# A two-layer sequence block and a mixture of experts on one core: six of eight xbc blocks in three passes, first taps on ScalarE, other work moved around them

## The chip, the cores and the metric

The kernel runs on one core of a Trainium2 chip. The metric is the device time of one execution in microseconds; the time before is the median of 3 runs. The engines are TensorE (matmul, here PE), VectorE (DVE), ScalarE (ACT), GpSimd (POOL) and SyncE (SP), which issues the weight loads.

## The reference

```python
for i in range(DEPTH):                                   # DEPTH = 2, SEQ = 256, D_MODEL = 1024
    x = x + 0.5 * swiglu(rms_norm(x, ffn1_norm[i]), ...)
    h = rms_norm(x, mix_norm[i])
    proj = h @ w_in[i]
    z, xbc, dt_raw, q, k, v = jnp.split(proj, splits, axis=-1)
    xbc = jax.nn.silu(causal_depthwise_conv(xbc, conv_w[i], conv_b[i]))   # 4 taps, 2048 channels
    y_ssd = ssd_mixer(xbc, dt_raw, z, dt_bias[i], a_log[i], d_skip[i], ssd_norm[i])
    ...
    y_att = dilated_attention(q, k, v).reshape(b, s, ATT_WIDTH)
    x = x + jnp.concatenate([y_ssd, y_att], axis=-1) @ w_out[i]
    x = x + 0.5 * swiglu(rms_norm(x, ffn2_norm[i]), ...)
# then a second block: mod = silu(c) @ w_ada (8 pieces of 1024), a gated linear attention with a
# convolution branch, and 32 experts of width 512 of which each token takes two
```

All values are float32. `ssd_mixer` takes step sizes `dt = softplus(dt_raw + dt_bias)`, turns them into decays and scans two chunks of 128 tokens.

## The kernel before

Activations lie transposed in SBUF: 128 channels on the partitions, 256 tokens along the row. A weight block is 1024 x 256, 1 MB, in one of four ring slots (`ring`). SyncE loads the block four places on as soon as TensorE has counted `freed` for the slot. The four PSUM banks of `misc` are taken in turn by every "fill"; `claim_bank` waits until the bank's last content is `drained`. Each engine works its own list of instructions in order, and the lists are written out by hand in one function for each engine.

**Two ways to multiply.** `cols_out` (line 930) multiplies a float32 block by `xnT` in one product; the trace shows it as two records for each 128 x 128 weight tile. The other way, in `three` (lines 779 to 781), splits both sides into a high part in fp32r and the rest: high by low, low by high, high by high. For that ScalarE copies the block into a high part (`high_w_block`, line 1810; three homes in turn, so a copy waits until the block three before has been read) and VectorE subtracts it from the block into `ring_low` (`low_w_block`, line 2390). The activations need `xh` (line 1802) and `xl` (line 2410).

**The xbc stage.** Behind the norm TensorE computes eight blocks of xbc (16 chunks of 128 channels). With `X_SPLIT = 4` blocks 0 to 3 go by `cols_out`, 4 to 7 by three passes; block 7 carries the step sizes dt beside it (line 993). Then come z's first block, the turns of x to tokens (line 1003, 16 transposes in four banks), the turns of B (line 1008), two more blocks of z, the cumulative decays (lines 1015, 1016, they wait for `adt_ready`), z's last block and the q, k and v blocks.

VectorE scales each evacuated xbc block by `row_rstd` (line 2416) and convolves four chunks at a time (a quartet, q = 0 to 3): the first tap with the bias (line 2426), then three taps of four instructions (line 2432). ScalarE takes the SiLU of a finished quartet (`conv_silu`, line 1814). Behind the last quartet VectorE reads dt (line 2445), which drains its bank, and ScalarE evacuates z's first block (line 1819), copies the token turns (line 1841), and takes Exp and Ln of the step sizes (lines 1849, 1852).

**Modulation pieces.** GpSimd sums eight pieces of `mod` over the stretch of the feed-forward blocks; `modulation(p)` on TensorE is 16 records with one column each (line 1164), and VectorE adds the bias (line 2642). In layer 0's second feed-forward block pieces 2 and 3 stand ahead of the last `down`, in layer 1's two blocks one piece each. The last `down` sums its two column halves one after the other and tells VectorE of the first (`acc_half`), which adds both to x (`add_x`, line 2374). Behind it TensorE turns x for the next norm (line 801).

## Time and profile before

| | |
|---|---|
| median of 3 runs | 2113.42 us (2113.1 to 2113.86) |
| the profiled execution | 2112.5 us, its span 2110.7 us |
| TensorE busy | 2069.4 us, 98% |
| VectorE busy | 1642.4 us, 78% |
| ScalarE busy | 1179.5 us, 56% |
| GpSimd busy | 454.9 us, 22% |

Times in the rows are microseconds from the start of the span. The xbc stage runs from 201.7 to 266.8 in layer 0 and from 834.9 to 898.2 in layer 1. Matmuls overlap, so their pace is read from start to start and not from their durations.

### The profile page before, as it was taken

The numbers are of one execution on the slowest core, as the hardware profiler recorded it, in microseconds if no ns is written. First come the engines' busy times: TensorE is split into PE (matmuls) and PEld (weight loads), VectorE is DVE, ScalarE is ACT, GpSimd is POOL, SyncE is SP. The second block draws the span as 40 slices with busy tenths as digits, with TensorE's granted clock in tenths as the row PEclk, the third lists the DMA queues.
The fourth block names the chain that finished last, engine by engine and source line by source line (L and its number), as shares of the span: only waits on it lengthen the run. The fifth ranks groups of instructions, "written<-read, shape, count | busy, mean of one in ns | idle before, by whom it ended". The sixth has DMA issues, their size and how long they took to land. (4 is left out here: it accounts for less than half of the span.)

```text
span 2110.7 us, 35271 instructions
## 1 busy us (share of the span) xinstructions
PE 2069.4 (98%) x13609; PEld 1845.2 (87%) x13609; DVE 1642.4 (78%) x2095; ACT 1179.5 (56%) x1483; POOL 454.9 (22%) x237
## 2 busy tenths in 40 slices
PE   9999999999999999999999999999999999999997
PEld 8998999789999998999789998999877878777775
DVE  5775867567766875867567766888699999999998
ACT  5433365653435433365653435344378888888886
POOL 4991000007931990000007930000000000000000
PEclk9999999999999999999999999999999999999999
DMA  8874554247765774554347753445669999999994
GB/s 261 282 253 159 160 160 141 100 142 243 265 226 164 266 257 152 163 154 140 101 143 244 265 184 120 132 125 174 243 231 369 366 372 368 375 370 372 374 369 180
DMA packets 238936, 483.66 MB, mean 229 GB/s; under 512 B 10612, under 2 KB 178976, under 8 KB 222464
## 3 DMA queue, kind: packets, MB, share of 16 engines
q1 hardware_dynamic: 226880, 443.58, 60.0%
q0 software_dynamic: 11360, 37.21, 5.3%
q10 hardware_dynamic: 608, 1.65, 0.2%
q8 instruction: 60, 0.98, 0.2%
q14 instruction: 28, 0.23, 0.0%
HBM read 481.31 MB, written 1.09 MB: 229 GB/s over the span
## 5 line engine op out<-in xcount | busy, mean ns | idle before, releaser
L780 PE MATMUL misc<-xh,ring_low 128*128 128x256 f32 x1472 | 407.4, 277 | 0.0
L779 PE MATMUL misc<-xl,high_b 128*128 128x256 f32 x1344 | 372.7, 277 | 0.0
L781 PE MATMUL misc<-xh,high_b 128*128 128x256 f32 x1344 | 371.8, 277 | 0.0
L2998 DVE TENSOR_TENSOR ring_low<-ring,high_b 128x2048 fp32r<-128x2048 f32 x128 | 287.1, 2284 | 0.6 <-issue 0.6
L780 PEld LDWEIGHTS misc<-xh,ring_low 128*128 128x128 f32 x1472 | 277.0, 188 | 3.5
L1766 ACT ACTIVATE arena<-arena 128x256 f32<-128x256 f32 x88 | 36.8, 419 | 416.9 <-DVE arena L2343 416.9
L2306 DVE TENSOR_TENSOR ring_low<-ring,high_b 128x2048 fp32r<-128x2048 f32 x88 | 255.6, 2940 | 9.3 <-ACT high_b L1735 8.7
L779 PEld LDWEIGHTS misc<-xl,high_b 128*128 128x128 f32 x1344 | 252.3, 188 | 3.4
L781 PEld LDWEIGHTS misc<-xh,high_b 128*128 128x128 f32 x1344 | 252.4, 188 | 0.0
L2056 ACT ACTIVATE high_b<-ring 128x2048 fp32r<-128x2048 f32 x124 | 235.7, 1914 | 27.8 <-DMA ring<-in_w_dram 26.9
L1648 POOL TENSOR_SCALAR arena<-arena,cact 128x1024 f32<-128x1024 f32 x56 | 213.0, 3804 | 3.9 <-DMA arena<-in_w_ada_dram 0.9
L1412 PE MATMUL misc<-high_b,ue 128*128 128x512 f32 x512 | 204.2, 399 | 1.9 <-DVE ue L3041 1.2
L1414 PE MATMUL misc<-ring_low,ue 128*128 128x512 f32 x512 | 199.9, 390 | 0.0
L1645 POOL TENSOR_SCALAR arena<-arena,cact 128x1024 f32<-128x1024 f32 x4 | 14.9, 3719 | 731.4 <-DVE hidl L2328 724.3
L1735 ACT ACTIVATE high_b<-ring 128x2048 fp32r<-128x2048 f32 x88 | 163.5, 1904 | 6.3 <-DMA ring<-in_ffn_w_up_dram 4.5
L779 PE MATMUL misc<-ring_low,xh 128*128 128x256 f32 x512 | 146.0, 285 | 2.4 <-DVE arena L2486 2.4
L3004 DVE TENSOR_TENSOR ring_d_low<-ring_d,high_r 128x1024 fp32r<-128x1024 f32 x128 | 147.9, 1215 | 0.5
L2343 DVE TENSOR_TENSOR arena<-misc,row_rstd 128x256 f32<-128x256 f32 x88 | 37.0, 421 | 136.1 <-PE misc L781 125.5
L781 PE MATMUL acc<-high_r,hidh 128*128 128x512 f32 x352 | 139.6, 397 | 0.0
L2061 ACT ACTIVATE high_r<-ring_d 128x1024 fp32r<-128x1024 f32 x128 | 131.6, 1055 | 14.0 <-DMA ring_d<-in_w_dram 13.3
L780 PE MATMUL acc<-high_r,hidl 128*128 128x512 f32 x352 | 139.0, 395 | 0.0
L779 PE MATMUL acc<-ring_d_low,hidh 128*128 128x512 f32 x352 | 138.3, 393 | 0.0
(474 smaller groups left out, 5092.7 us busy)
## 6 DMA issues: line engine op xcount, KB each, us to landing
ring<-in_w_dram SPq DMA_DIRECT2D x128, 1024.0 KB, 7.7
ring<-in_w_in_dram SPq DMA_DIRECT2D x72, 1024.0 KB, 5.5
ring_d<-in_w_dram SPq DMA_DIRECT2D x128, 512.0 KB, 5.2
ring<-in_ffn_w_gate_dram SPq DMA_DIRECT2D x44, 1024.0 KB, 5.5
ring<-in_ffn_w_up_dram SPq DMA_DIRECT2D x44, 1024.0 KB, 8.9
ring_d<-in_ffn_w_down_dram SPq DMA_DIRECT2D x88, 512.0 KB, 7.5
arena<-in_w_ada_dram POOLq DMA_DIRECT2D x48, 512.0 KB, 5.1
ring<-in_w_out_dram SPq DMA_DIRECT2D x20, 1024.0 KB, 4.8
```

Source lines behind the costliest of these rows:

```text
L779: pe.matmul(dst, wh, ml, start=start, stop=False, **kw)
L780: pe.matmul(dst, wl, mh, start=False, stop=False, **kw)
L781: return pe.matmul(dst, wh, mh, start=False, stop=stop, **kw)
L1412: pe.matmul(b, ue[:, k, half, :], expert_part(high_b, x)[:, kk, :], start=(k == 0), stop=False)
L1414: mm = pe.matmul(b, ue[:, k, half, :], expert_part(ring_low, x)[:, kk, :], start=False, stop=(k == KD - 1))
L1648: pool.tensor_scalar(row, row, cact[:, k:k + 1], None, ALU.mult).then_inc(pool_step, 1)
L1735: act.activation(high_b[:, s, :], ring[:, s, :], ACT.Copy).then_inc(high_in[s], 1)
L2056: act.activation(high_b[:, s, :], ring[:, s, :], ACT.Copy).then_inc(high_in[s], 1)
L2061: act.activation(high_r[:, s, :], ring_d[:, s, :], ACT.Copy).then_inc(high_in_d[s], 1)
L2306: dve.tensor_tensor(ring_low[:, s, :], ring[:, s, :], high_b[:, s, :].bitcast(F32), ALU.subtract)\
L2998: dve.tensor_tensor(ring_low[:, s, :], ring[:, s, :], high_b[:, s, :].bitcast(F32), ALU.subtract)\
L3004: dve.tensor_tensor(ring_d_low[:, s, :], ring_d[:, s, :], high_r[:, s, :].bitcast(F32), ALU.subtract).then_inc(low_in_d[s], 1)
```

## The change

`X_SPLIT` becomes 6: xbc blocks 2 to 7 go in three passes. ScalarE makes `xh` and the high parts of blocks 2 and 3 (b = -6 and -5) before it loads the table for SiLU and copies `row_rstd`, and it takes the first tap with the bias of each quartet (`first_taps`), counted in a new semaphore `tap_in`, for which VectorE's other three taps wait. The order of VectorE's list is written anew: `xl` first, a low part behind each evacuation, the taps behind each second one; the reading of dt and `dn` stand ahead of the last quartet. ScalarE's last `conv_silu` moves behind z's first block and the token copies. Of two modulation pieces the second moves between the halves of the last `down`, on TensorE and on VectorE.

```diff
-        X_SPLIT = 4
+        X_SPLIT = 6
         SPLIT = [(RING[k], uses) for k, uses in slots if k[0] == "ffn" or k == "moe"]
         SPLIT += [(RING["win", l] + 8 - X_SPLIT, 16 + X_SPLIT) for l in range(DEPTH)]
...
-            def down(m0, n0, d0, g0, i, c, start, stop):
+            def down(m0, n0, d0, g0, i, c, start, stop, between=()):
...
                     if stop and (t, cc) == (1, 0):
                         mm.then_inc(acc_half, 1)
+                        for p in between:
+                            modulation(p)
                 mm.then_inc(freed_d[dn % SLOTS], 1)
...
-                for p in pieces:
+                for p in pieces[:1]:
                     modulation(p)
-                down(m0, n0, d0, NF * f, 0, NF - 1, False, True)
+                down(m0, n0, d0, NF * f, 0, NF - 1, False, True, pieces[1:])
...
                 n0 = RING["win", l]
                 root_of_squares(3 * l + 1)
-                rms(3 * l + 1, ACT.Silu)
-                act.wait_ge(rstd_ready, 3 * l + 2)
                 for q in range(4):
                     wait_drained(act, FILL["norm", 3 * l + 1] + q)
                 act.activation(xh[:, :, :], xnT[:, :, :], ACT.Copy).then_inc(xs_high, 1)
+                wait_summed(act, ROWD["ffn", 2 * l], 0, NF - 2)
+                wait_summed(act, ROWD["ffn", 2 * l], 0, NF - 1)
+                for b in (-6, -5):
+                    n = n0 + 8 + b
+                    act.wait_ge(loaded[n % SLOTS], LOAD * (n // SLOTS + 1))
+                    act.activation(high_w(b), ring[:, n % SLOTS, :], ACT.Copy).then_inc(high_in[n % SLOTS], 1)
+                rms(3 * l + 1, ACT.Silu)
+                act.wait_ge(rstd_ready, 3 * l + 2)
 
...
-                for j in range(8):
-                    wait_slot_read(act, n0 + j)
-                    if j < 3:
-                        high_w_block(j - 4)
-                    if j >= 4:
-                        high_w_block(j - 5)
-                    if j in (3, 5, 7):
-                        conv_silu(j // 2 - 1)
-                conv_silu(3)
+                def first_taps(q):
+                    for j in range(2 * q, 2 * q + 2):
+                        wait_drained(act, FILL["xbc", l] + j)
+                    for ch in range(4 * q, 4 * q + 4):
+                        at_ = C_CW + (CONV_K - 1) * NX + ch
+                        ins = act.activation(xc[:, ch, :], xraw[:, ch, CONV_K - 1:], ACT.Identity,
+                                             scale=cola[:, l, at_:at_ + 1], bias=cola[:, l, C_CB + ch:C_CB + ch + 1])
+                    ins.then_inc(tap_in, 1)
+
+                wait_slot_read(act, n0)
+                high_w_block(-4)
+                first_taps(0)
+                wait_slot_read(act, n0 + 1)
+                high_w_block(-3)
+                conv_silu(0)
+                wait_slot_read(act, n0 + 2)
+                high_w_block(-2)
+                first_taps(1)
+                wait_slot_read(act, n0 + 3)
+                high_w_block(-1)
+                conv_silu(1)
+                wait_slot_read(act, n0 + 4)
+                high_w_block(0)
+                first_taps(2)
+                wait_slot_read(act, n0 + 5)
+                high_w_block(1)
+                conv_silu(2)
+                wait_slot_read(act, n0 + 6)
+                first_taps(3)
+                high_w_block(2)
 
                 def z_out_of(j):
                     block_out(FILL["z", l, j], j, z[:, :, j * BLK:(j + 1) * BLK], ACT.Silu)
@@ -1840,6 +1870,7 @@
                     wait_filled(act, m)
                     act.activation(xtok[:, t, half * 512:(half + 1) * 512], bank_of(m), ACT.Copy)\
                         .then_inc(drained[m % 4], 1)
+                conv_silu(3)
                 m = FILL["bt", l]
                 wait_filled(act, m)
                 act.activation(btok.rearrange("p a b -> p (a b)"), bank_of(m), ACT.Copy)\
@@ -2358,14 +2389,16 @@
...
-                for p in pieces:
+                for p in pieces[:1]:
                     modulation(p)
-                add_x(u + 1, lambda t: half_rstd[:, t:t + 1], lambda: wait_summed(dve, d0, 0, NF - 1))
-
-            def add_x(u, factor, wait_last):
+                add_x(u + 1, lambda t: half_rstd[:, t:t + 1], lambda: wait_summed(dve, d0, 0, NF - 1), pieces[1:])
+
+            def add_x(u, factor, wait_last, between=()):
 
                 for c in range(2):
                     if c:
+                        for p in between:
+                            modulation(p)
                         wait_last()
                     else:
                         dve.wait_ge(acc_half, u)
...
-                for q in range(NX // 4):
-                    if q == 3:
-                        low_w_block(0)
-                    chunks = range(4 * q, 4 * q + 4)
-                    if q == 0:
-                        dve.wait_ge(row_ready, 3 * l + 2)
-                    if q == 2:
-                        low_w_block(-2)
-                    for j in range(2 * q, 2 * q + 2):
-                        if j == 1:
-                            dve.wait_ge(xs_high, l + 1)
-                            dve.tensor_tensor(xl[:, :, :], xnT[:, :, :], xh[:, :, :].bitcast(F32), ALU.subtract)\
-                                .then_inc(xs_low, 1)
-                        if j == 3:
-                            low_w_block(-3)
-                        m = FILL["xbc", l] + j
-                        wait_slot_read(dve, n0 + j)
-                        dve.tensor_tensor(xraw[:, 2 * j:2 * j + 2, CONV_K - 1:],
-                                          bank_of(m).rearrange("p (a b) -> p a b", a=2),
-                                          row_rstd[:, :].unsqueeze(1).to_broadcast([P, 2, SEQ]), ALU.mult)\
-                            .then_inc(drained[m % 4], 1)
+                dve.wait_ge(xs_high, l + 1)
+                dve.tensor_tensor(xl[:, :, :], xnT[:, :, :], xh[:, :, :].bitcast(F32), ALU.subtract)\
+                    .then_inc(xs_low, 1)
+                low_w_block(-6)
+
+                def raw(j):
+                    m = FILL["xbc", l] + j
+                    wait_slot_read(dve, n0 + j)
+                    dve.tensor_tensor(xraw[:, 2 * j:2 * j + 2, CONV_K - 1:],
+                                      bank_of(m).rearrange("p (a b) -> p a b", a=2),
+                                      row_rstd[:, :].unsqueeze(1).to_broadcast([P, 2, SEQ]), ALU.mult)\
+                        .then_inc(drained[m % 4], 1)
+
+                def convolve(q):
                     for j in range(2):
                         wait_drained(dve, FILL["xbc", l] + 2 * q + j)
-                    if q == 2:
-                        low_w_block(-1)
+                    dve.wait_ge(tap_in, 4 * l + q + 1)
                     last = {}
-                    for ch in chunks:
-                        last[ch] = step(dve.tensor_scalar(
-                            xc[:, ch, :], xraw[:, ch, CONV_K - 1:], taps(ch)(CONV_K - 1),
-                            cola[:, l, C_CB + ch:C_CB + ch + 1], ALU.mult, ALU.add))
                     for k in range(CONV_K - 1):
-                        for ch in chunks:
-                            after_step(last[ch])
+                        for ch in range(4 * q, 4 * q + 4):
+                            if k:
+                                after_step(last[ch])
                             ins = dve.scalar_tensor_tensor(out=xc[:, ch, :], in0=xraw[:, ch, k:k + SEQ],
                                                            scalar=taps(ch)(k), in1=xc[:, ch, :],
                                                            op0=ALU.mult, op1=ALU.add)
@@ -2436,9 +2458,26 @@
                                 last[ch] = step(ins)
                             else:
                                 ins.then_inc(conv_done, 1)
-                    if q == 0:
...
+
+                dve.wait_ge(row_ready, 3 * l + 2)
+                raw(0)
+                low_w_block(-5)
+                raw(1)
+                low_w_block(-4)
+                convolve(0)
+                raw(2)
+                low_w_block(-3)
+                raw(3)
+                low_w_block(-2)
+                convolve(1)
+                raw(4)
+                low_w_block(-1)
+                raw(5)
+                low_w_block(0)
+                convolve(2)
+                raw(6)
+                low_w_block(1)
+                raw(7)
                 m = FILL["dt", l]
                 wait_filled(dve, m)
...
                 wait_drained(dve, m)
                 dve.scalar_tensor_tensor(out=dn, in0=dr, scalar=-1.0, in1=dr, op0=ALU.mult, op1=ALU.min)\
                     .then_inc(dn_ready, 1)
-                for j in range(1, 4):
+                convolve(3)
+                for j in range(2, 4):
                     low_w_block(j)
                 dve.wait_ge(dl_ready, l + 1)
                 link(dve.scalar_tensor_tensor(out=dtv, in0=dr, scalar=0.0, in1=dl, op0=ALU.max, op1=ALU.add))
```

## Rows read from the trace of the kernel before

**Rows 1.** The page, section 1: busy time of each engine.
```profile
PE 2069.4 (98%) x13609; PEld 1845.2 (87%) x13609; DVE 1642.4 (78%) x2095; ACT 1179.5 (56%) x1483; POOL 454.9 (22%) x237
```
**Rows 2.** Windows: us; PE, PEld, DVE, ACT, POOL busy; granted clock; DMA share; GB/s.
```profile
202.00:205.50 3.50, 3.50 (x10) 2.77 (x9) 0.32 (x3) 2.38 (x5) 0.00 (x0) 0.52 0.00 0
636.10:639.00 2.90, 2.90 (x28) 2.89 (x26) 2.49 (x2) 2.88 (x3) 0.00 (x0) 1.00 0.98 336
639.10:645.80 6.70, 6.70 (x21) 5.43 (x21) 2.27 (x6) 1.38 (x2) 0.00 (x0) 0.50 0.68 236
827.00:836.00 9.00, 8.29 (x53) 6.97 (x52) 5.92 (x11) 3.41 (x7) 0.00 (x0) 1.00 0.74 231
```
**Rows 3.** Timeline of PE (start, us, what), pieces 2 and 3, layer 0.
```profile
635.87 0.39 PE L781 MATMUL acc<-high_r,hidh 128*128 128x512 f32 x1
636.10 1.84 PE L1164 MATMUL misc<-ones,arena 128*128 128x1 f32 x16
637.80 2.42 PE L1164 MATMUL misc<-ones,ada 128*128 128x1 f32 x16
...
641.51 0.63 PE L779 MATMUL acc<-ring_d_low,hidh 128*128 128x512 f32 x1
...
645.35 1.30 PE L801 MATMUL misc<-konst,x 128*128 128x128 f32 x8
```
**Rows 4.** Timeline of PE, the single piece of layer 1.
```profile
827.47 1.84 PE L1164 MATMUL misc<-ones,arena 128*128 128x1 f32 x16
```
**Rows 5.** Timeline of DVE, layer 0: the second half added to x.
```profile
645.59 1.41 DVE L2374 SCALAR_TENSOR_TENSOR x<-acc,stat,x 128x512 f32<-128x512 f32 x2 [1.08 <-PE acc L781]
```
**Rows 6.** Timeline of PE in the xbc stage of layer 1.
```profile
842.27 20.89 PE L930 MATMUL misc<-xnT,ring 128*128 128x256 f32 x96
862.80 0.47 PE L779 MATMUL misc<-xl,ue 128*128 128x256 f32 x1
...
879.67 0.29 PE L993 MATMUL misc<-wdt,xnT 128*128 128x16 f32 x2
...
894.05 1.03 PE L1003 MATMUL misc<-konst,arena 128*128 128x128 f32 x8
895.64 0.66 PE L1003 MATMUL misc<-konst,arena 128*128 128x128 f32 x4 [0.56 <-DVE arena L2445]
897.17 0.66 PE L1003 MATMUL misc<-konst,arena 128*128 128x128 f32 x4 [0.87 <-ACT arena L1819]
...
909.62 0.30 PE L1015 MATMUL misc<-arena,konst 128*128 128x32 f32 x2
```
**Rows 7.** Timeline of DVE in the same stage: evacuation, first tap, taps, low part.
```profile
872.24 0.68 DVE L2416 TENSOR_TENSOR arena<-misc,row_rstd 128x512 f32<-128x512 f32 x1
...
877.08 1.38 DVE L2426 TENSOR_SCALAR arena<-arena,cola 128x256 f32<-128x256 f32 x4
878.37 4.84 DVE L2432 SCALAR_TENSOR_TENSOR arena<-arena,cola 128x256 f32<-128x256 f32 x12
883.13 2.28 DVE L2390 TENSOR_TENSOR ring_low<-ring,ring_d_low 128x2048 fp32r<-128x2048 f32 x1
```
**Rows 8.** Timeline of ACT in the same stage.
```profile
837.94 1.28 ACT L1725 ACT_TABLE_LOAD   x1
...
879.58 1.92 ACT L1810 ACTIVATE ring_d_low<-ring 128x2048 fp32r<-128x2048 f32 x1 [2.54 <-PE misc L781]
...
904.30 0.23 ACT L1852 ACTIVATE arena<-arena 128x32 f32<-128x32 f32 x1
```
**Rows 9.** Line 1751, Identity on ScalarE: ns min/median/max, starts, form.
```profile
L1751 ACT ACTIVATE xnT<-misc,mod,gains x4: 557/566/570, 1279.7 to 1281.0; 128x256 f32<-128x256 f32 x4
```
**Rows 10.** The page, section 6: loads of w_in, KB each, median us to landing.
```profile
ring<-in_w_in_dram SPq DMA_DIRECT2D x72, 1024.0 KB, 5.5
```
**Rows 11.** GpSimd in layer 1's stage (windows), two low parts beside GpSimd (timeline).
```profile
834.00:930.00 96.00, 92.86 (x686) 88.67 (x687) 68.03 (x105) 47.06 (x55) 0.00 (x0) 1.00 0.47 143
...
596.34 6.68 DVE L2306 TENSOR_TENSOR ring_low<-ring,high_b 128x2048 fp32r<-128x2048 f32 x2
```

More of the change, by code:

```diff
@@ L425, in two_blocks @@
         xc_ready = sem("xc_ready")
+        tap_in = sem("tap_in")
         z_ready = sem("z_ready")
@@ L2438, in ssd_and_projections @@
                                 ins.then_inc(conv_done, 1)
-                    if q == 0:
-                        low_w_block(-4)
+                dve.wait_ge(row_ready, 3 * l + 2)
[17 more added lines that the diff above has]
+                raw(7)
                 m = FILL["dt", l]
```

## The prediction

> **What bounds the kernel now.** I read the page first: TensorE is busy for 98% of the span [rows 1]. Next I asked for the granted clock of single stretches, because a busy TensorE at half clock does half the work. Then came TensorE in order of time around the two places that the change touches, and last VectorE, ScalarE, the loads and GpSimd there, to see how far ahead of TensorE they run. Two things stand out.
>
> First, in the feed-forward block before layer 1, TensorE runs modulation(2) and modulation(3) back to back, 32 products of one column each. Behind them the clock is at half: 1.00 granted from 636.1 to 639.0, 0.50 from 639.1 to 645.8, that is 1.2 instead of 2.4 GHz [rows 2]. TensorE counts as busy all through this, so the waits don't show it. The spacing of matmuls does: the last nine of the down product take from 641.51 to 645.35, 0.43 us each, against 0.23 us ahead of the pieces [rows 3].
>
> Second, the xbc stage (the same in both layers; I use layer 1). Three blocks in one product take from 842.27 to 862.80, 6.84 us each. Then 147 matmuls of three-pass blocks take from 862.80 to 879.67, less 0.2 us before the second of them: 0.1135 us each, 5.45 us for a block's 48 [rows 6]. A three-pass block is the cheaper one, if its parts are ready. Behind z's first block come the turns to tokens, and two of them stand: the third four start 1.59 us after the first eight, which need 8 x 0.109 = 0.87, and the fourth four 1.53 us after the third, which need some 0.48. That is 0.7 and 1.05 us, 1.75 together. The rows name VectorE's step sizes (L2445) and ScalarE's z (L1819) as releasers [rows 6]: both stand in their queues behind the last taps.
>
> **The change, part by part.**
>
> *Piece 3 between the halves.* TensorE's instructions stay as they are; the order becomes piece 2, half, piece 3, half. At full clock a piece takes 1.70 us, from 636.10 to 637.80 [rows 3], and the twelve down matmuls 12 x 0.23 = 2.75 us plus about 0.1 us after each piece: 1.70 + 1.70 + 2.95 = 6.35 us, against the 9.25 us from 636.10 to 645.35 [rows 3]. Gain 2.9 us, if the clock stays up. The nearest row with a piece ahead of a down product and the turns after it is in layer 1, one piece from 827.47 on, down halves and turns behind it: 1.00 granted from 827 to 836 [rows 2, 4]. Two pieces with half a down product between them lie between that and the pair that fell, and nearer to the single piece, since dense work stands on each side of each piece. What is late next is x's second half: VectorE adds it at 645.59, 0.24 us behind 645.35, where the last product gives way to the turns [rows 3, 5]. It moves with that product, so the gain passes on whole. VectorE's own modulation(3) stands in front of that add, but piece 3 ends 1.4 us before it. In the other three feed-forward blocks nothing moves.
>
> *Blocks 2 and 3 in three passes.* Each saves 6.84 - 5.45 = 1.39 us of TensorE, 2.8 us for a layer [rows 6]. What must hide: ScalarE copies two more blocks (1.92 us each) and VectorE subtracts two more (2.28 us each) [rows 7, 8]. ScalarE makes its two ahead of row_rstd, right behind xh: three copies of about 1.85 us from 837.9 on, then the table load that stands at 837.94 before [rows 8], so row_rstd comes near 845.3 instead of 842.9. VectorE's first evacuation waits for it, and frees a bank that TensorE wants at about 860: nothing. VectorE has the first low part at 844.5 and the second at 848.4; TensorE wants them at 849.2 and 854.6.
>
> *First taps to ScalarE.* VectorE is relieved of 1.3 us for four chunks, from 877.08 to 878.37 [rows 7]. For two blocks it then has two evacuations of 0.6, two low parts of 2.2 and twelve taps in 4.75 us (starts to starts [rows 7]), 10.35 us, and TensorE takes 2 x 5.45 = 10.9. With the first taps kept it would be 11.65, and VectorE would be the bound. ScalarE's new instruction, Identity with a scale and a bias from memory, has its form in the second block's norm: 566 ns from PSUM [rows 9], 2.3 us for four and the upper bound; the lower is Ln's 0.23 us on a tile of 32 columns [rows 8], 0.9 us. I take 1.9, near the upper, whose row has the same shape and kinds of operands; either end changes only how long VectorE waits for tap_in. For two blocks ScalarE has 3.7 + 1.9 + 1.0 = 6.6 us of 10.9: free. A new wait arises: VectorE's taps wait for tap_in, and behind them stand the next evacuations and low parts.
>
> I followed the three queues through layer 1 by these durations, a load landing 5.5 us after its slot is free [rows 10]. Low parts are ready, against TensorE's want: block 4 at 852.3 for 860.1, block 5 at 859.9 for 865.6, block 6 at 864.6 for 871, block 7 at 872.2 for 876.5, z0 at 875.6 for 885.4, z1 at 883.2 for 893.5, z2 at 895.3 for 899.2. VectorE waits a few tenths for tap_in, 1.5 us in the last quartet. The smallest slack is some 4 us, at block 7 and z2. No new stall.
>
> *Step sizes and turns ahead of the last taps.* VectorE reads dt right after its last evacuation, near 886.6; ScalarE evacuates z's first block as soon as it ends (891.1 to 892.1), the last SiLU comes after the token copies. The third four turns (from 892.0) find their bank free, the fourth (from 892.4) too: the 1.75 us go. What is late next: ScalarE's Exp and Ln stand behind the copy of block 11. In the kernel before, Ln ends at 904.53 [rows 8], now near 900.8. adt is ready 0.5 us later; TensorE wanted it at 909.62 [rows 6] and now at 905.0: 3.6 us are left. The last chunks' SiLU at 895.1 is wanted behind z3, at 911. Nothing new.
>
> Sum for a layer: 2.8 + 1.75 = 4.5 us, twice 9.1; with 2.9 for the pieces 12.0 us. Later stages load and copy when TensorE frees a slot, so they move with it and should keep their time. The profiled execution took 2112.5 us (span 2110.7): 2100.5. The median of the runs is 0.9 us above it: **2101.4 us**.
>
> **Rivals.**
>
> *The clock falls all the same.* Behind the second half come sixteen transposes with a wait for x, as in layer 1 (832.4 to 835). For: in layer 0 one piece between transposes and a plain block went with 0.52 granted from 202.0 to 205.5 [rows 2]. Against: layer 1's single piece. A fall costs half of 3.5 to 6.7 us, 1.7 to 3.3: 2103 to 2105. The Trainium skill ("TensorE: Matmul & The Clock Gate", Part 4: PE-mode transpose) says that transposes don't count as busy work for the clock in the way that products do. By that rule the stretch behind piece 3 is thin, and this rival is what happens; layer 1's stretch with the same transposes, at 1.00, speaks against it. The same page (HAM oscillation) ties a fall to gaps in which TensorE is idle; the fall at 639 came with no gap at all, so here the trace decides.
>
> *The queues bite.* VectorE has only 10.9 - 10.35 = 0.55 us to spare for two blocks, and each wait for tap_in or for a copy (which waits for TensorE to read the block three before) eats of it. If waits of 2.5 us came in every quartet, VectorE would fall back by 1.95 us for each two blocks, 6.8 us from block 2 to z's first, 2.8 more than the slack of 4, and what the three passes save in a layer would go: 2101.4 + 5.6 = 2107.
>
> *Slower.* One mechanism: GpSimd working beside VectorE in the xbc stage. Two low parts that overlap GpSimd take 6.68 us from 596.34 [rows 11] instead of 4.5, so up to 4.4 for one against 2.2. At that pace two blocks cost VectorE 14.8 us against TensorE's 10.9, 3.9 behind for each pair, 13.6 over the 3.5 pairs to z's first block, 9.1 after a slack of 4.5, and 18 for both layers: 2119. It turns the sign at 6 us for a layer, that is where a low part takes more than some 4.0 us. Against: GpSimd has 0.00 us in the whole stretch [rows 11], and its next pieces are gated by feed-forward chunks.
>
> *Nothing in the end.* The stretch after the stage is set by VectorE or ScalarE and takes back what TensorE gained in the xbc stage: then the pieces alone remain, 2110.5, within 0.2%. For: adt's slack is only 3.6 us. Against: a copy there starts when TensorE has read a slot, so a TensorE that comes earlier is followed earlier; the only fixed chain is Exp and Ln, and it keeps its slack.
>
> **How the numbers follow.** Forecast 2101.4, 0.70, with 2099 to 2103.5 as its own range: a fall of the clock at the start of layer 0 can last 3.5 us or none, and a new wait of some tenths may stand at each of a dozen places. Clock falls 0.10, queues 0.12, nothing 0.05, slower 0.03. From 2098.5 to 2106 the forecast, the clock's case and part of the queues' are held. 0.2% is 4.2 us, about what a measurement of this kernel can tell from no change: faster than 2109.2 are the first three, 0.92; same 0.05; slower 0.03.
>
> **What would show it.** In the profile after: granted clock 1.00 from the first of the two pieces to the next gate product, and twelve down matmuls 0.23 us apart; plain blocks only two, from the third on 48 matmuls with 0.1135 us, no idle time before the first of block 2 to 7; no wait of the turns for L2445's or L1819's successors; z1 beginning 4.5 us earlier against block 0; VectorE with short waits for the new taps; Identity at 0.4 to 0.6 us without a table load. It would be wrong if TensorE waits for low parts, if adt comes after z2, or if 0.50 stands behind the pieces.

## The result and the profile after

The changed kernel takes 2101.41 us (median of four executions, 2098.96 to 2106.97) beside 2113.57 us for the kernel before (2113.10 to 2113.86): 0.9949 of it, 95% interval 0.9934 to 0.9964. The forecast was 2101.4 us, with 2099 to 2103.5 as its own range and 2098.5 to 2106 as the range held in all. The profiled execution of the changed kernel is its longest, 2106.97 us with a span of 2105.2.

The first line is the page's busy time (as [rows 1]), under it stretches from the windows view: us, busy time of PE, PEld, DVE, ACT and POOL, granted clock, DMA share, GB/s.

```profile
PE 2065.6 (98%) x13673; PEld 1847.7 (88%) x13673; DVE 1641.5 (78%) x2067; ACT 1203.2 (57%) x1519; POOL 455.8 (22%) x237
...
202.00:205.50 3.50, 3.50 (x19) 3.14 (x20) 0.53 (x4) 3.47 (x7) 0.00 (x0) 1.00 0.00 0
631.45:637.80 6.35, 6.35 (x46) 5.78 (x44) 4.65 (x6) 4.37 (x4) 0.00 (x0) 1.00 1.07 355
637.80:644.00 6.20, 5.21 (x40) 4.56 (x39) 5.68 (x11) 5.25 (x13) 0.00 (x0) 1.00 0.39 139
1269.80:1276.60 6.80, 6.80 (x22) 3.44 (x22) 1.43 (x4) 0.00 (x0) 1.16 (x2) 0.50 0.04 9
1515.60:1525.80 10.20, 10.20 (x50) 10.20 (x50) 5.44 (x20) 6.85 (x9) 0.92 (x2) 0.50 0.60 243
```

The clock stays at 1.00 through both pieces and behind them, where it fell before [rows 2]. It is also at 1.00 at 202, where the kernel before fell and where the change moves nothing on TensorE. And it falls, to 1.2 GHz, at 1269.8 and 1515.6, in parts of the program that the change doesn't touch. Such falls are one part of the scatter between executions and not all of it: the mean granted clock of seven executions of the kernel before, among thirty on one chip, was 0.994, and they took from 2112.1 to 2128.3 us.

The pieces in order of time (TensorE; answers [rows 3]):

```profile
631.45 1.84 PE L1167 MATMUL misc<-ones,arena 128*128 128x1 f32 x16
633.15 0.48 PE L780 MATMUL acc<-ring_d_low,hidh 128*128 128x512 f32 x1
...
634.62 1.84 PE L1167 MATMUL misc<-ones,ada 128*128 128x1 f32 x16
636.32 0.48 PE L780 MATMUL acc<-ring_d_low,hidh 128*128 128x512 f32 x1
...
637.80 1.03 PE L802 MATMUL misc<-konst,x 128*128 128x128 f32 x8
```

From 631.45 to 637.80 are 6.35 us, where [rows 3] have 9.25. The xbc stage of layer 1 on TensorE (answers [rows 6]):

```profile
834.23 0.61 PE L825 MATMUL acc<-konst,stat 128*128 128x128 f32 x4
834.67 7.07 PE L933 MATMUL misc<-xnT,ring 128*128 128x256 f32 x32
...
841.39 0.47 PE L780 MATMUL misc<-xl,ring_d_low 128*128 128x256 f32 x1
...
883.52 1.91 PE L1006 MATMUL misc<-konst,arena 128*128 128x128 f32 x16
885.26 0.60 PE L1011 MATMUL misc<-konst,arena 128*128 128x128 f32 x4
885.67 0.36 PE L780 MATMUL misc<-ring_low,xh 128*128 128x256 f32 x1
...
897.06 0.30 PE L1018 MATMUL misc<-arena,konst 128*128 128x32 f32 x2
```

One plain block is left behind the row of 1/rms (L825), and the sixteen turns (L1006) run in one group without a wait: 2.15 us from the first of them to z's next block, 4.19 before. VectorE and then ScalarE in the same stage (timelines; answer [rows 7, 8]):

```profile
863.27 2.28 DVE L2423 TENSOR_TENSOR ring_low<-ring,ue 128x2048 fp32r<-128x2048 f32 x1
...
873.22 0.69 DVE L2440 TENSOR_TENSOR arena<-misc,row_rstd 128x512 f32<-128x512 f32 x1
...
880.86 4.85 DVE L2454 SCALAR_TENSOR_TENSOR arena<-arena,cola 128x256 f32<-128x256 f32 x12 [1.82 <-ACT arena L1837]
...
893.17 0.26 DVE L2499 SCALAR_TENSOR_TENSOR arena<-arena 128x16 f32<-128x16 f32 x2
```

```profile
835.74 1.28 ACT L1728 ACT_TABLE_LOAD   x1
...
866.25 2.08 ACT L1837 ACTIVATE arena<-arena,cola 128x256 f32<-128x256 f32 x4 [0.59 <-DVE arena L2440]
...
878.64 2.08 ACT L1837 ACTIVATE arena<-arena,cola 128x256 f32<-128x256 f32 x4 [4.24 <-DVE arena L2440]
```

Four first taps (L1837) take 2.08 us and bring no table load. VectorE waits 1.82 us for them in the last quartet. TensorE doesn't see it.

### The profile page after: what moved, and what is told of

Same layout as the page of the kernel before. It is cut to its first block and busy times, and to the rows that moved or that the text cites. A ratio compares the mean times of both kernels' runs of the same rounds, so it can differ in the third digit from the quotient of the medians.

```text
span 2105.2 us, 35451 instructions
## 1 busy us (share of the span) xinstructions
PE 2065.6 (98%) x13673; PEld 1847.7 (88%) x13673; DVE 1641.5 (78%) x2067; ACT 1203.2 (57%) x1519; POOL 455.8 (22%) x237
## 5 line engine op out<-in xcount | busy, mean ns | idle before, releaser
L781 PE MATMUL misc<-xh,ring_low 128*128 128x256 f32 x1536 | 425.6, 277 | 0.0
L781 PEld LDWEIGHTS misc<-xh,ring_low 128*128 128x128 f32 x1536 | 289.4, 188 | 3.4
L1415 PE MATMUL misc<-high_b,ue 128*128 128x512 f32 x512 | 203.8, 398 | 2.7 <-DVE ue L3081 1.2
L2092 ACT ACTIVATE high_r<-ring_d 128x1024 fp32r<-128x1024 f32 x128 | 131.8, 1055 | 13.8 <-DMA ring_d<-in_w_dram 12.6
```

Source lines behind the costliest of these rows:

```text
L781: pe.matmul(dst, wl, mh, start=False, stop=False, **kw)
L1415: pe.matmul(b, ue[:, k, half, :], expert_part(high_b, x)[:, kk, :], start=(k == 0), stop=False)
L2092: act.activation(high_r[:, s, :], ring_d[:, s, :], ACT.Copy).then_inc(high_in_d[s], 1)
```

## The experiments

**How they are compared.** Single executions of one kernel scatter by 5 to 19 us here, more than most parts of the change are worth. So besides the medians I read every profile at the same marks, the starts of rows on TensorE: the row of 1/rms (L825 in the rows above), the first dt product (L996), the cumulative decays (L1018). "Stage" is from the first to the second, "turns" from the second to the third (z's blocks and the turns), "feed-forward" from the row of 1/rms of layer 0's second feed-forward block to that of layer 1's first, which holds the two pieces.

Lengths of 34.9 and 36.0 us for one kernel are no misprint; the last section comes to them.

| profile | feed-forward | stage, layers 0/1 | turns, layers 0/1 | half clock at (for us), tail of the program left out |
|---|---|---|---|---|
| before | 191.4 | 37.9 / 37.8 | 29.5 / 30.0 | 14.4, 202.2, 1284.2 (3.4 each), 639.1 (6.8) |
| before, again | 190.4 | 37.8 / 38.5 | 29.5 / 30.1 | 15.1, 202.8, 639.7 (3.4 each) |
| pieces alone | 188.5 | 38.5 / 38.5 | 29.7 / 30.1 | none |
| stage alone | 189.7 | 34.9 / 36.0 | 27.9 / 28.1 | 200.6 (6.8), 637.5 (3.4) |
| changed | 188.7 | 36.0 / 34.9 | 27.9 / 27.9 | 13.7 (3.4), 1269.8 (6.8), 1515.6 (10.2) |
| changed, again | 188.5 | 34.9 / 36.0 | 27.9 / 28.1 | 13.5 (3.4) |
| changed, third | 188.5 | 34.9 / 36.0 | 27.9 / 28.1 | 203.6, 1517.7 (3.4 each), 1272.0 (6.8) |
| order put back | 188.5 | 36.0 / 34.9 | 32.2 / 31.6 | 13.4, 266.0, 894.1 (3.4 each), 201.2 (6.8) |
| four passes again | 188.4 | 38.5 / 37.8 | 27.9 / 27.9 | 201.2, 1276.4 (3.4 each) |
| first taps on VectorE | 188.5 | 34.9 / 34.9 | 27.9 / 27.9 | 15.2, 203.0, 1271.3 (3.4 each) |
| the same, again | 188.5 | 34.9 / 36.0 | 27.9 / 28.1 | none |
| seven blocks | 188.5 | 33.4 / 34.7 | 27.9 / 28.1 | 14.1, 205.3, 1277.1 (3.4 each) |
| seven blocks, again | 188.5 | 34.7 / 34.7 | 27.9 / 27.9 | 13.8, 201.6, 1269.9 (3.4 each) |
| seven, piece moved | 192.6 | 34.7 / 33.4 | 29.7 / 27.9 | 14.6 (3.4) |

In the last line the 29.7 of layer 0 holds the moved piece.

**1. The changed kernel again** (no edit).

> The changed kernel as it is, for more executions of it. Its four executions so far lie from 2099.0 to 2107.0 us, where the four of the kernel before lie from 2113.1 to 2113.9; the profiled one (2107.0) lost about 4 us at one fall of the granted clock at 1515.6 us, behind the second layer's last w_out2 work, where the kernel before has none. Theory 1 (the change takes 12 us everywhere, and the falls of the clock lie in other places from one execution to the next): the median lies at 2100 to 2102, single executions spread over 5 to 8 us, and the new profile shows its falls at other times than 1269.8 and 1515.6. Theory 2 (the new order itself brings a fall at 1515): the profile shows it there again and the median lies at 2103 or more.

2099.87 us (2098.24 to 2106.29), the kernel before on the same chip 2113.11 (2107.73 to 2118.88): 0.9944, 0.9929 to 0.9960. The profile has no fall between 17 us and the program's tail: theory 1. The order does not bring the fall at 1515 each time.

**2. The pieces alone**, on the kernel before.

```diff
-                for p in pieces:
+                for p in pieces[:1]:
                     modulation(p)
-                down(m0, n0, d0, NF * f, 0, NF - 1, False, True)
+                down(m0, n0, d0, NF * f, 0, NF - 1, False, True, pieces[1:])
```

> The kernel before with one part of the change alone: the second piece of the next w_in work stands between the two down halves, the third stays behind. Theory 1 (this move takes away the clock's fall at 639 us, and only that): 2.9 us less than before, 2110.7, and a granted clock of 1.0 over 636 to 650 us. Theory 2 (what fell at 639 falls somewhere else, in the router or the stage behind it): 2112.5 to 2114, with a new fall of 3 us or more behind 645 us in the profile. Theory 3 (the half behind piece 2 waits for the hidden layer): under 1.5 us less, and a wait of TensorE on the down half.

2111.78 us, 1.3 below the 2113.11 beside it; ratio 0.9997, 0.9984 to 1.0009, so by the times alone it can't be told from nothing. In the profile the fall is gone and the feed-forward has 188.5 us, with no fall behind it: theory 1 by the profile, open by the time.

**3. The stage alone**: the changed kernel with `pieces` as before.

> The changed kernel with the pieces put back as they were, both together ahead of the last down half: the change of the xbc stage alone. Theory 1 (the parts add up): 9.1 us less than before, 2104.4, with the piece 2, piece 3 and half rows as in the kernel before (start of the last half behind both pieces) and a fall of the clock near 636 us. Theory 2 (the xbc stage's gain is smaller than its sum, and the pieces gave more): 2106 or more. Theory 3 (the fall at 639 does not come back, since falls lie anywhere): 2101 to 2102 and a clock of 1.0 there.

2102.19 us: 10.9 below the kernel before, 2.3 above the changed kernel. The fall is back at 637.5, for 3.4 us, and the feed-forward has 189.7. None of the three theories hit the time (2104.4, over 2106, 2101 to 2102); the profile is theory 1's.

```profile
637.50:640.90 3.40, 3.40 (x12) 2.62 (x11) 1.83 (x3) 0.00 (x0) 0.00 (x0) 0.51 0.72 255
```

**4. The kernel before, again** (no edit).

> The kernel before once more, for a second profile of it: where the granted clock falls. Theory 1 (the two pieces side by side make the fall at 639 us, in every execution): a fall of 3.4 to 6.8 us between 634 and 642 us again, while those at 14, 202 and 1284 may be absent or elsewhere. Theory 2 (falls lie anywhere): none there. Time 2108 to 2119 us, as its 23 executions on this chip.

2112.65 us. The fall behind the pieces is there, for 3.4 us where the first profile had 6.8, as theory 1 has it:

```profile
639.70:643.10 3.40, 3.40 (x11) 2.82 (x12) 0.46 (x3) 1.19 (x2) 0.00 (x0) 0.50 1.10 363
```

Together: side by side, the pieces are followed by a fall in three profiles of three; apart, in none of eleven. What the move is worth is the fall's length: 191.4, 190.4 and 189.7 us against 188.5, that is 2.9, 1.9 and 1.2 us, 2.0 on average.

**5. The order at the end of the stage put back.**

```diff
                 raw(7)
+                convolve(3)
                 m = FILL["dt", l]
 ...
-                convolve(3)
                 for j in range(2, 4):
@@ ScalarE
                 first_taps(3)
                 high_w_block(2)
+                conv_silu(3)
                 def z_out_of(j):
 ...
-                conv_silu(3)
                 m = FILL["bt", l]
```

> The changed kernel with the order at the end of the stage put back: VectorE convolves the last quartet ahead of reading the dt rows and the step sizes, and ScalarE reads the last silus ahead of z and of the token turns. Theory 1 (the order alone ends TensorE's two waits in the stage, 0.9 us and 0.87 us in each layer, while the three passes and the first taps give the rest): 3.5 us more than the changed kernel, 2105, with a wait of TensorE on the turns or the cumulative sums again in each layer. Theory 2 (the first taps on ScalarE have already taken the last quartet off VectorE, so that the order gives nothing more): within 1 us of the changed kernel.

2107.77 us, 7.9 above the changed kernel of experiment 1, over twice what theory 1 gave. TensorE in layer 1:

```profile
890.61 1.04 PE L1006 MATMUL misc<-konst,arena 128*128 128x128 f32 x8
893.14 0.66 PE L1006 MATMUL misc<-konst,arena 128*128 128x128 f32 x4 [1.49 <-DVE arena L2485]
894.66 1.11 PE L1006 MATMUL misc<-konst,arena 128*128 128x128 f32 x4 [0.87 <-ACT arena L1828]
...
896.28 0.56 PE L780 MATMUL misc<-ring_low,xh 128*128 128x256 f32 x1
```

From the first turn to z's next block are 5.67 us, 3.5 more than changed and 1.5 more than before. TensorE waits 1.49 us for the step sizes where [rows 6] have 0.56. Here is VectorE in layer 1, first in the kernel before, then in this one:

```profile
888.37 0.69 DVE L2416 TENSOR_TENSOR arena<-misc,row_rstd 128x512 f32<-128x512 f32 x1 [2.35 <-PE misc L781]
889.17 1.38 DVE L2426 TENSOR_SCALAR arena<-arena,cola 128x256 f32<-128x256 f32 x4
...
895.21 0.37 DVE L2445 SCALAR_TENSOR_TENSOR arena<-misc,stat,heads 128x16 f32<-128x16 f32 x2
```

```profile
884.93 0.69 DVE L2440 TENSOR_TENSOR arena<-misc,row_rstd 128x512 f32<-128x512 f32 x1 [1.73 <-PE misc L782]
887.95 4.84 DVE L2454 SCALAR_TENSOR_TENSOR arena<-arena,cola 128x256 f32<-128x256 f32 x12 [2.33 <-ACT arena L1837]
892.72 0.37 DVE L2485 SCALAR_TENSOR_TENSOR arena<-misc,stat,heads 128x16 f32<-128x16 f32 x2
```

In both VectorE stands ready and evacuates block 7 as soon as TensorE ends it, and from there TensorE has the same 5.7 us to the turns (888.37 to 894.05, 884.93 to 890.61). A TensorE that comes earlier thus takes the last quartet along. What grew is VectorE's way from that evacuation to the step sizes, 6.84 us before and 7.79 here: it stands idle for 2.33 us until ScalarE has taken the first taps, where its own first taps took 1.3. That is the 0.93 us by which TensorE waits longer (1.49 against 0.56).

In this profile the clock also falls in the second wait of either layer, at 266.0 and 894.1. No other profile has a fall there. The last eight turns of layer 1 and their gap to z's block take 1.62 us at half clock, 1.07 before (897.17 to 898.24), so I estimate that 5.1 of the 5.67 us would remain at full clock, 3.0 more than changed. With the falls the column "turns" is 4.3 us longer in layer 0 and 3.7 in layer 1, together the 7.9.

**6. Blocks 2 and 3 in four passes again** (`X_SPLIT = 4`, without their copies and low parts).

> The changed kernel with blocks 2 and 3 in four full-precision passes again, first taps and order as changed. Theory 1 (the three passes are worth what their products are: 6.84 us against 5.45 us a block, four blocks): 5.6 us more than the changed kernel, 2105.5. Theory 2 (the time of the stage is set by VectorE and ScalarE, so that faster blocks only wait): under 3 us more.

2107.32 us beside 2112.89 for the kernel before; no changed kernel ran beside this one, against the 2099.9 to 2101.4 of its three medians it is 5.9 to 7.5 more. Its stage takes 37.8 us in layer 1, as in the kernel before, and 38.5 in layer 0: theory 1. The three passes are worth 2.9 us a layer where TensorE runs at the faster of its two paces (37.8 against 34.9) and 2.5 at the slower (38.5 against 36.0).

**7. The first taps on VectorE**, twice (VectorE's part of the edit; on ScalarE the four calls of `first_taps` go).

```diff
-                    dve.wait_ge(tap_in, 4 * l + q + 1)
                     last = {}
+                    for ch in range(4 * q, 4 * q + 4):
+                        last[ch] = step(dve.tensor_scalar(
+                            xc[:, ch, :], xraw[:, ch, CONV_K - 1:], taps(ch)(CONV_K - 1),
+                            cola[:, l, C_CB + ch:C_CB + ch + 1], ALU.mult, ALU.add))
```

> The changed kernel with the first taps back on VectorE (four products a quartet there, none on ScalarE), order and three passes kept. Theory 1 (VectorE's work for two blocks goes from 10.5 us to 12 us, over the 10.9 us that TensorE takes for them, and VectorE becomes the bound of the stage): TensorE waits for a low part or a bank in blocks 5 to 7 and at the turns, 2 to 5 us more than the changed kernel, 2102 to 2105. Theory 2 (VectorE's waits in the stage, 2.5 us for ScalarE's copies at a time, take the work in): within 1 us of the changed kernel, no wait of TensorE in the stage.

> The changed kernel with the first taps on VectorE, again, beside the changed kernel. Its first profile (2099.5 us) showed no wait of TensorE in the stage and the changed kernel's durations, 34.9 us and 27.9 us; but the median of its twelve executions was 2105.2. Theory 1 (with the order and three passes in place the first taps' engine does not matter, and the median was the chip of that call): within 1.5 us of the changed kernel. Theory 2 (in most executions VectorE is late, and the profiled one was the lucky one): 3 us or more above it, and a wait of TensorE in the stage of this profile.

The first time 2105.19 us (before beside it: 2112.89), the second 2097.78, with the changed kernel beside it at 2100.69. The medians point in opposite ways: the first is 3.8 to 5.3 us above the three medians of the changed kernel, none of which was taken beside it, and the second is 2.9 us below the one beside it, which neither of its theories has. Both profiles have the changed kernel's lengths in every column, and no wait of TensorE on VectorE or ScalarE between the row of 1/rms and the decays. So in this stage the first taps' engine doesn't matter by the marks (theory 2 of the first expectation); the times leave it open. Why the twelve executions of the first run came out higher I can't say; its profiled one (2099.5) was the lowest of them. VectorE in layer 1 of the second:

```profile
862.92 0.68 DVE L2436 TENSOR_TENSOR arena<-misc,row_rstd 128x512 f32<-128x512 f32 x1
863.52 2.28 DVE L2419 TENSOR_TENSOR ring_low<-ring,ue 128x2048 fp32r<-128x2048 f32 x1
...
874.56 0.68 DVE L2436 TENSOR_TENSOR arena<-misc,row_rstd 128x512 f32<-128x512 f32 x1
```

The pair takes 11.64 us, more than TensorE's 10.9, and yet block 7's low part ends at 865.80 for a block that starts at 868.47. In the first of the two profiles the same stage ran at the faster pace. Its low part of block 7 (VectorE) and block 7's first product (TensorE):

```profile
865.29 2.28 DVE L2419 TENSOR_TENSOR ring_low<-ring,ue 128x2048 fp32r<-128x2048 f32 x1
```

```profile
869.28 0.28 PE L780 MATMUL misc<-xl,ue 128*128 128x256 f32 x1
```

The low part ends 1.7 us ahead of the block, where the changed kernel at the same pace has 3.3 (865.55 for 868.80).

**8. Seven blocks in three passes**, twice, the second time beside the changed kernel.

```diff
-        X_SPLIT = 6
+        X_SPLIT = 7
@@ ScalarE, ffn, behind chunk NF - 2 of a block ahead of an xbc stage (VectorE: the same place, the low part)
+                            act.activation(high_w(-7), ring[:, n % SLOTS, :], ACT.Copy).then_inc(high_in[n % SLOTS], 1)
@@ ScalarE, root_of_squares(3 * l + 1), which is given to=z
-                    s = step(act.activation(xsc[:, t, :], x[:, t, :], ACT.Square, accum_out=ss[:, t:t + 1]))
+                    s = step(act.activation(to[:, t, :], x[:, t, :], ACT.Square, accum_out=ss[:, t:t + 1]))
```

> The changed kernel with block 1 of each layer's xbc stage in three passes as well (seven of eight). Its weights are high-copied and differenced behind the last but one chunk of the feed-forward before it, where ScalarE is idle from 809.8 to 816.7 us and VectorE from 811.3 to 816.2; the squares' junk output goes to the free z rows so that the copy can stand in their old place. Theory 1 (a block in three passes gives the same again, since VectorE's low part of x ends at 833.42 us, just when block 1 starts at 833.57): 1.6 us less a layer, 3.2 us less than the changed kernel, 2096.7 to 2098. Theory 2 (VectorE, at 10.5 us of work for each pair of blocks of 10.9 us, becomes the bound once the stage starts earlier): under 1 us less, and waits of TensorE for a low part in the stage.

> Seven blocks of eight in three passes, again, beside the changed kernel. Its first profile showed block 1 shorter by 1.5 us in each layer and no wait of TensorE for a low part, but 3.1 us lost to the slower pace over the first feed-forward and two falls more of the clock. Theory 1 (pace and falls are chance, the block is worth 1.5 us a layer): 3 us less than the changed kernel of the same call. Theory 2 (the extra copy and difference in the feed-forward bring the slower pace and the falls with them): no less than the changed kernel, the slow pace over 20 to 196 us again.

> The changed kernel again, as the measure for the three beside it on the same chip. 2100 to 2102; from its row of 1/rms in layer 1 to the dt products 34.9 us if TensorE runs its three-pass products at 0.1135 us each, 36.0 us if at 0.118, as the profiles so far show the one or the other.

The first time 2099.43 us (before beside it 2112.89; 0.9924, 0.9896 to 0.9952). That is 0.4 to 2.0 us below the three medians of the changed kernel, none of which was taken beside it, less than theory 1 of the first expectation has. The second time 2097.61 beside 2100.69 for the changed kernel: 3.1 less, as theory 1 of both says. (The changed kernel beside it shows 34.9 us in layer 0 and 36.0 in layer 1, one pace in each.) The copy and the low part cost nothing where they stand in layer 1: from the row of 1/rms of its first feed-forward block to that of its xbc stage are 187.5 us in this profile and in the changed kernel's beside it (ScalarE, then VectorE, then TensorE in layer 1):

```profile
810.76 1.90 ACT L1786 ACTIVATE ue<-ring 128x2048 fp32r<-128x2048 f32 x1
```

```profile
812.70 2.29 DVE L2397 TENSOR_TENSOR ring_low<-ring,ue 128x2048 fp32r<-128x2048 f32 x1 [0.41 <-ACT ue L1786]
...
832.15 2.29 DVE L2442 TENSOR_TENSOR xl<-xnT,xh 128x2048 fp32r<-128x2048 f32 x1 [1.42 <-ACT xh L1807]
```

```profile
834.15 0.61 PE L825 MATMUL acc<-konst,stat 128*128 128x128 f32 x4
834.51 0.37 PE L780 MATMUL misc<-xl,ue 128*128 128x256 f32 x1
...
868.88 0.29 PE L996 MATMUL misc<-wdt,xnT 128*128 128x16 f32 x2
```

The low part of x ends at 834.44 us and the first three-pass product starts at 834.51: an eighth block would have to wait (that wasn't tried). The block is worth 1.5 us at the faster pace (33.4 against 34.9) and 1.3 at the slower (34.7 against 36.0).

**9. Seven blocks, and layer 0's first piece moved** between z's blocks 1 and 2.

```diff
-                if not l:
-                    modulation(0)
                 ssd_and_projections(l, 4 * l + 1)
 ... (VectorE's modulation(0) and the order of the fills move likewise)
                 project(l, FILL["z", l, 1], 1)
+                if not l:
+                    modulation(0)
```

> Seven blocks in three passes, and layer 0's first piece of the modulation (sixteen one-column products, 1.92 us) moved from just ahead of block 0 of the xbc stage to between the z blocks 1 and 2. In seven of the ten profiles so far the clock falls at 200 to 205 us, some us behind these products; layer 1 has none there and no fall at that place. Theory 1 (one-column products next to the turns and their waits bring the fall, as the two pieces at 639 did, three profiles of three with them side by side and none of seven with them apart): no fall between 198 and 206 us nor near 265, 1.5 to 2.5 us less than seven blocks alone. Theory 2 (the fall comes from the turns and waits alone): a fall near 200 us in the profile, and at most 0.5 us less.

2096.88 us (2094.22 to 2102.31; 0.9934 of the kernel before, 0.9917 to 0.9952), 0.7 below seven blocks: not told apart from it by the times, and theory 1's 1.5 to 2.5 us are not reached. The profile shows what theory 1 says of the clock: it is at 1.00 from 196 to 285, and TensorE goes from the turns into block 0 with a wait of 0.52 us between:

```profile
197.21 2.29 PE L802 MATMUL misc<-konst,x 128*128 128x128 f32 x16
200.02 4.34 PE L933 MATMUL misc<-xnT,ring 128*128 128x256 f32 x19 [0.52 <-ACT xnT L1756]
```

With the piece ahead of block 0, nine profiles of thirteen have a fall at 200 to 206; here there is none, and layer 1, which has no piece there, has none in any. One profile can't prove it: by chance a fall would be missing in four of thirteen.

## Why the prediction was right, step by step

- **The pieces.** The order takes the predicted 6.35 us to the hundredth, and the clock stays up. The size is the part that came out wrong: it was read off one execution whose fall happened to last 6.8 us, and over three profiles the term is 2.0 us instead of 2.9. The clock rival (it falls all the same) did not come true in any of eleven profiles; layer 1's single piece was the right neighbour to argue from. By the rule that I took from the Trainium skill ("TensorE: Matmul & The Clock Gate", Part 4), that transposes don't keep the clock up, the sixteen behind piece 3 should have brought it down; at this place the trace doesn't bear it out (1.00 from 637.80 to 644.00 above).
- **Three passes.** Predicted 2.8 us a layer, found 2.9 at the faster pace (37.8 to 34.9, and back to 37.8 in experiment 6) and 2.5 at the slower. That TensorE has a second pace the prediction did not know.
- **Turns.** Predicted 1.75 us a layer, found 1.7 and 2.0 (29.5 to 27.9, 30.0 to 27.9). It is the order that does it: the column keeps its 27.9 us without the three passes (experiment 6) and with the first taps on VectorE (experiment 7), and only the old order lengthens it. But 1.75 is what the order takes away from the kernel before. With the first taps on ScalarE the old order would cost some 3.0 us a layer, the falls of the clock left out (experiment 5): VectorE's last quartet then waits for ScalarE. I had not asked what my own second part would do to this very wait.
- **Slack.** The queues that I followed came out close. Block 7's low part: 865.55 for 868.80, 3.3 us (predicted 4.3). adt: ready at 893.43, wanted at 897.06, 3.6 (3.6). Four first taps: 2.08 us (1.9). Wait for them in the last quartet: 1.82 (1.5). The rivals of the queues, of GpSimd and of "nothing in the end" did not come true.
- **First taps on ScalarE: the wrong step.** I wrote that with them on VectorE "VectorE would be the bound", 11.65 against 10.9 us for a pair. The 11.65 is right (11.64 measured), the conclusion is not. There are only some four pairs, the low parts of blocks 2 to 7 run 3 to 8 us ahead in the changed kernel, and part of VectorE's added work only fills its idle time: between its evacuations of blocks 1 and 7 it stands idle for 4.3 us with the first taps on ScalarE and for 1.8 with its own (first profile of experiment 7, same pace). The rest comes out of the lead, which is 1.7 us at block 7 instead of 3.3. This part of the diff is worth nothing that these runs can show, and with the old order of experiment 5 it costs 0.9 us in layer 1.
- **The sum.** 2.0 + 2 x 4.8 = 11.6 us by the marks at the faster pace, 12.0 predicted, and 12.2, 13.2 and 10.3 by the medians of the three comparisons. That the first median hit within 0.1 us is luck: executions of the changed kernel alone run from 2098 to 2107.
- **The profiled execution** is 5.5 us below the one before and not 12. At layer 1's decays it is 12.6 ahead (909.6 to 897.1), at the first product of L1296 behind the second layer 13.7 (1282.6 to 1268.9), at the first expert product (L1415) 7.3 (1548.1 to 1540.8), at the last product 5.5 (2098.4 to 2092.9). The 6.4 us between the second and the third of these marks go with the two long stretches at half clock, 1269.8 and 1515.6, against one of 3.4 us before. Between the third and the last, 1.7 us went with no fall at all; what took them stays open.

## What to carry to other kernels

A rate of one engine over another is a bound only if the stretch is long enough to use up the lead: work out lead divided by deficit before calling an engine the bound. An order fix must be priced against the kernel as it will be: work handed to another engine brings a wait of its own (2.33 us here for 1.3 us of work), and where that wait stands on the path to the next step, the same order costs more. And where executions scatter by more than a part is worth, cut profiles at common marks: at one pace 188.5 and 27.9 us repeat to some 0.2 us where the changed kernel's medians move by 1.5.

## What was not expected of the hardware

- **Falls of the clock differ from one execution to the next.** Of fourteen profiles two have none ahead of the program's tail and one has 20.4 us of it, most in the same five places. None lies inside long dense stretches; all follow short products (one-column pieces, turns, the router) or waits.
- **A second pace at full clock.** Three-pass products of 256 columns run 0.1135 us apart in one stretch and 0.118 in the next, at a granted clock of 1.00 both times, and in the xbc stage which it is changes between executions: the stage takes 34.9 or 36.0 us in the same kernel. It isn't all chance: from 290 to 315 and from 910 to 935 us, where z's last block and the q and k blocks run, all fourteen profiles have 0.118. One whole feed-forward ran at the slower pace in experiment 9 and took 192.6 us instead of 188.5. The first row below is the changed kernel's third profile, the second is experiment 9's; between the same times the second holds 1069 recorded products instead of 1101:

```profile
470.00:620.00 150.00, 150.00 (x1101) 141.15 (x1101) 112.91 (x109) 57.16 (x54) 107.17 (x46) 1.00 0.74 250
```

```profile
470.00:620.00 150.00, 150.00 (x1069) 140.78 (x1068) 114.24 (x108) 57.15 (x54) 109.59 (x46) 1.00 0.71 241
```

The pace mostly changes from one stage to the next, but not only: in the first profile of experiment 8 it went from 0.1135 to 0.118 in the middle of layer 0's first feed-forward, near 85 us, and stayed there. What sets it stays open.
